# Two modulation vectors of the first attention: summed by TensorE from the weights in the ring instead of by VectorE

## The chip, the cores and the metric

The kernel runs on one core of one Trainium2 chip. The metric is the device time of one execution in microseconds, as the median of several runs. The engines are TensorE (PE, with its weight loads as PEld), VectorE (DVE), ScalarE (ACT), GpSimd (POOL) and SyncE (SP), which issues the weight DMAs.

## The reference

A sequence of 256 tokens of width 1024 goes through three layers. Each begins with an adaptive norm: a conditioning vector `c` times a weight matrix gives shift, scale and gate. What matters here is layer 0's attention (`nsa_mixer`) and the norm of layer 1 behind it.

```python
def adaln_norm(x, c, g, w_ada, b_ada):
    mod = jax.nn.silu(c) @ w_ada + b_ada
    shift, scale, gate = jnp.split(mod, 3, axis=-1)
    h = rms_norm(x, g) * (1.0 + scale[:, None, :]) + shift[:, None, :]
    return h, gate[:, None, :]
...
    o = gates[..., 0:1] * o_cmp + gates[..., 1:2] * o_slc + gates[..., 2:3] * o_win
    o = o.reshape(B, T, ATTN_WIDTH)
    return (o * jax.nn.silu(z)) @ w_out
```

The product `silu(c) @ w_ada` has one row. The kernel cuts it into 30 vectors of 512 columns ("ada" 0 to 29, six for each of five norms); ada 6 to 9 are shift and scale of the second norm.

## The kernel before, in words

**Weights.** SP brings every weight into a ring of six slots of 128 x 1024 float32 (512 KB), in the order of `plan.units`, and issues a load when the slot's former unit has been used. A weight of a large product is split by ACT (rounded part, the CAST) and DVE or POOL (rest, the subtraction), and TensorE makes three products from the parts: L574, L576 and L589, each 128 x 128 weights on 512 columns. In this text "a product" is one of these.

**Modulation vectors.** A vector takes four ring units of two 128-row chunks. `ada_step` does one chunk on DVE: ring times a scalar of `c_act`, added into the accumulator `ada_acc` (L698 for the first chunk, L704 for the others). After eight steps `ada_sum` on TensorE adds the accumulator over the partitions with four matmuls against a column of ones (L735). `ada_collect` on DVE then adds bias and gain. Vector 3 alone is made in another way: `ada_direct` multiplies 128 x 128 blocks of the ring, as stationary weights, by one column of `c_act` on TensorE (L757), two chunks for each of four column groups of each unit. A float32 matmul that is no transpose stands in the trace as two records, each with a weight load.

**The first attention** (`Attention`, with 32 items: 16 heads, two branches) goes in 16 pairs. In step p TensorE makes the scores of pair p (L1167, L1169), turns the probabilities of the two items of pair p-1 (L1176, three transposes each), weighs the values of pair p-2 (L1187 to L1189), and puts in products of the output gate ("nsa", 5), 28 of 48 over the attention; 20 are kept for behind it. DVE masks the scores and takes their maximum (L1218, L1220, from PSUM), makes the bias (L1199), copies every second turned item (L664), does ada steps, and every second step weighs a group of four (L1251, L1445, L1450). ACT makes the exponentials (L1244, L1246) and the other copies. POOL adds groups (L1608) and subtracts for the units of ("nsa", 5) (L533). Of the 32 ada steps of vectors 6 to 9, twelve are done ahead of the attention and twenty in it.

**Behind it** `by_halves` on TensorE takes the 20 kept products, turns the attention's output, and makes the first half of the output projection ("nsa_out", 0), with `ada_sum` of vectors 6 to 9 between groups of eight products. DVE collects the four vectors, then takes the residual (L864), then subtracts for the last two units of ("nsa_out", 1) (L533), for which TensorE's L589 wait.

Of the kernel before, what the change touches and what calls it, by code (L numbers as in the profile page):

```python
# [12 lines left out]
P = 128  # L13
# [3 lines left out]
KC = D // P  # L17
# [98 lines left out]
ADA_ON_PE = (3,)  # L116
# [3 lines left out]
class Plan:  # L120


    def __init__(self, stages):
# [8 lines left out]
        for kind, key, lots, freers in stages:  # L132
# [3 lines left out]
            for i, dmas in enumerate(lots):  # L136
                if kind == "ada_mix":
                    consumer = "pe" if key[i] in ADA_ON_PE else "ada"
                elif kind in ("beside", "beside_more"):
                    consumer = "ada" if key[i][0] == "ada" else "split"  # L140
# [13 lines left out]
            elif kind in ("beside", "beside_more"):  # L154
                for name in dict.fromkeys(key):
                    mine = [u for u, m in zip(units, key) if m == name]
                    self.outputs[name] = (None if name[0] == "ada" else len(self.freers), mine)
                    if name[0] == "ada":
                        self.ada_at.update((u, name[1]) for u in mine)
# [64 lines left out]
def first_stages(A):  # L224
# [37 lines left out]
    s.append(beside([(("nsa", 5), w, 2304)], range(8, 10), 2))  # L262
# [99 lines left out]
def build(nc, A, const_ap, out, last_block=2):  # L362
    ctx = ExitStack()
    with ctx:
# [17 lines left out]
        mod_tmp = sb("mod_tmp", [P, 4])  # L382
        mod_scale = sb("mod_scale", [P, 5, KC])
# [74 lines left out]
        mod_ready = sem("mod_ready")  # L458
        dve_chain = sem("dve_chain")
        act_chain = sem("act_chain")  # L460
# [223 lines left out]
        def ada_step(n, kk):  # L684
# [4 lines left out]
            if n >= SUMS and kk == 0 and n - SUMS not in ADA_ON_PE:  # L689
                dve.wait_ge(ada_summed, n - SUMS + 1 - sum(a < n - SUMS for a in ADA_ON_PE))  # L690
# [19 lines left out]
        def ada_beside(n0, i):  # L710

            n, kk = n0 + i // 8, i % 8
# [12 lines left out]
        def ada_sum(pe, n):  # L725
# [3 lines left out]
            if n >= SUMS:  # L729
                pe.wait_ge(mod_ready, TOGETHER[n][0] if n in TOGETHER else n)  # L730
# [32 lines left out]

        collected = [0]

        def ada_collect_up_to(n):
            while collected[0] < n:
                ada_collect(collected[0])

        def ada_collect(n):  # L770

            dve, link = nc.vector, chain["dve"]
            assert collected[0] == n, n
# [3 lines left out]
            if n in ADA_ON_PE:  # L777
# [4 lines left out]
            else:  # L782
                last = TOGETHER[n][-1] if n in TOGETHER else n
                dve.wait_ge(ada_summed, last + 1 - sum(a < last for a in ADA_ON_PE))
# [4 lines left out]
            elif part < 4:  # L789
                gain = cols[:, 0, 16 + 8 * layer + half.start:16 + 8 * layer + half.stop]  # L790
                if n in TOGETHER:
                    dve.wait_ge(mod_ready, n)
# [63 lines left out]
        def residual_half_dve(dve, layer):  # L856

            stage = RESIDUALS[layer]
            for tt in range(TT):
# [3 lines left out]
                dve.wait_ge(mod_ready, 6 * layer + 5)  # L863
# [18 lines left out]
        def residual_tile_dve(dve, layer, tt):  # L882
# [4 lines left out]
            dve.wait_ge(mod_ready, 6 * layer + 6)  # L887
# [82 lines left out]
        def shift_left_act(act, layer, tt, h):  # L970
            name, b = f"norm{layer + 1}", 2 * tt + h
            act.wait_ge(mod_ready, 6 * layer + 10)
# [144 lines left out]
        class Attention:  # L1117
# [27 lines left out]
            def pe(self, pe, products, n_products, lead=0):  # L1145

                n, done = len(self.items), 0
                for p in range(self.steps + 2):
                    for part in range(4):
# [3 lines left out]
                        if part % 2 == 0 and 0 <= j < n:  # L1153
                            self.turn_probs(pe, j)
# [169 lines left out]
        def nsa_dve(dve, link):  # L1324
# [48 lines left out]
            def some_ada(n):  # L1373
                for _ in range(n):
                    ada_beside(6, ada_done[0])
# [91 lines left out]
            def ada_in_attention(i):  # L1467
                some_ada(n_before + (32 - n_before) * (i + 1) // 32 - ada_done[0])
# [1517 lines left out]
```

## Time and profile before

| what | value |
|---|---|
| median of three runs | 1240.8 us (1237.46 to 1241.46) |
| profiled execution, its own time | 1239.51 us |
| its span in the profile | 1237.7 us |
| mean granted TensorE clock | 0.977 of full |
| busy: PE, DVE, ACT, POOL | 92%, 71%, 44%, 12% |

Busy shares are means over the whole span. A row of a timeline gives the start, how long the instructions took together, and in brackets the idle time ahead of them with what ended it. Matmuls overlap, so what one costs is read from start to next start, not from its duration.

### The profile page before, as it was taken

The numbers are of one execution on the slowest core, as the hardware profiler recorded it, in microseconds if no ns is written. First come the engines' busy times: TensorE is split into PE (matmuls) and PEld (weight loads), VectorE is DVE, ScalarE is ACT, GpSimd is POOL, SyncE is SP. The second block draws the span as 40 slices with busy tenths as digits, with TensorE's granted clock in tenths as the row PEclk, the third lists the DMA queues.
The fourth block names the chain that finished last, engine by engine and source line by source line (L and its number), as shares of the span: only waits on it lengthen the run. The fifth ranks groups of instructions, "written<-read, shape, count | busy, mean of one in ns | idle before, by whom it ended". The sixth has DMA issues, their size and how long they took to land. (4 is left out here: it accounts for less than half of the span.)

```text
span 1237.7 us, 19929 instructions
## 1 busy us (share of the span) xinstructions
PE 1135.5 (92%) x7662; PEld 954.1 (77%) x7662; DVE 874.1 (71%) x1458; ACT 549.9 (44%) x989; POOL 152.3 (12%) x109
## 2 busy tenths in 40 slices
PE   6878899899898899999989999898988998999997
PEld 5657677777677688888878877787878876888886
DVE  5866798589786699965489946847576656855554
ACT  1333366433363634344477754433141435434542
POOL 0010131122331100000000002104033021000011
PEclk9988899999899999999999999998989999999999
DMA  8875343378654399976455552751102144955452
GB/s 321 288 269 196 112 136 121 109 227 293 219 190 137 106 325 328 342 241 187 153 173 178 169 186 90 249 189 36 37 1 72 59 152 153 318 186 185 160 199 69
DMA packets 143513, 221.63 MB, mean 179 GB/s; under 512 B 10855, under 2 KB 66747, under 8 KB 143291
## 3 DMA queue, kind: packets, MB, share of 16 engines
q1 hardware_dynamic: 140512, 216.37, 53.2%
q10 hardware_dynamic: 2907, 4.00, 0.9%
q8 instruction: 61, 1.00, 0.3%
q14 instruction: 33, 0.27, 0.1%
HBM read 219.28 MB, written 1.05 MB: 178 GB/s over the span
## 5 line engine op out<-in xcount | busy, mean ns | idle before, releaser
L533 DVE TENSOR_TENSOR w_parts<-ring,w_parts 128x1024 fp32r<-128x1024 f32 (+2 forms) x276 | 341.9, 1275 | 90.6 <-ACT w_parts L528 89.8
L528 ACT CAST w_parts<-ring 128x1024 fp32r<-128x1024 f32 (+2 forms) x288 | 290.0, 1036 | 259.6 <-PE bank L576 70.6
L574 PE MATMUL bank<-w_parts,lhs_hi 128*128 128x512 f32 (+2 forms) x960 | 385.2, 402 | 13.6 <-ACT w_parts L528 9.2
L576 PE MATMUL bank<-w_parts,lhs_lo 128*128 128x512 f32 (+2 forms) x960 | 377.2, 393 | 0.0
L589 PE MATMUL bank<-w_parts,lhs_hi 128*128 128x512 f32 (+2 forms) x960 | 266.6, 394 | 18.1 <-DVE w_parts L533 18.1
L589 PEld LDWEIGHTS bank<-w_parts,lhs_hi 128*128 128x128 f32 x960 | 180.4, 191 | 58.8 <-DVE w_parts L533 25.2
L574 PEld LDWEIGHTS bank<-w_parts,lhs_hi 128*128 128x128 f32 x960 | 184.3, 192 | 51.8 <-issue 13.2
L576 PEld LDWEIGHTS bank<-w_parts,lhs_lo 128*128 128x128 f32 x960 | 184.3, 192 | 32.3 <-issue 0.2
L704 DVE SCALAR_TENSOR_TENSOR ada_acc<-ring,c_act,ada_acc 128x512 f32<-128x512 f32 x203 | 168.7, 831 | 13.3 <-DMA ring<-in_ada_w 3.0
L574 PE MATMUL bank<-w_parts,up_hi 128*128 128x512 f32 x176 | 68.7, 390 | 0.0
L576 PE MATMUL bank<-w_parts,up_lo 128*128 128x512 f32 x176 | 68.5, 389 | 0.0
L873 POOL TENSOR_TENSOR x<-x,xn 128x512 f32<-128x512 f32 x10 | 17.6, 1780 | 403.5 <-DVE xn L864 403.5
L651 PE MATMUL bank<-const,arena 128*128 128x128 f32 (+2 forms) x318 | 45.4, 275 | 11.2 <-DVE arena L664 5.1
L651 PEld LDWEIGHTS bank<-const,arena 128*128 128x128 f32 (+2 forms) x318 | 36.7, 141 | 18.9 <-DVE arena L664 5.8
L589 PE MATMUL bank<-w_parts,up_hi 128*128 128x512 f32 x176 | 48.4, 390 | 0.0
L1913 DVE TENSOR_TENSOR arena<-arena,bank 128x256 f32<-128x256 f32 x44 | 17.5, 417 | 39.3 <-ACT arena L1925 39.0
L2031 DVE SCALAR_TENSOR_TENSOR arena<-arena,cols 128x256 f32<-128x256 f32 x96 | 42.2, 481 | 2.3 <-ACT arena L2021 0.8
L1925 ACT ACTIVATE arena<-bank 128x256 f32<-128x256 f32 x44 | 16.3, 382 | 58.8 <-PE bank L589 57.5
L533 POOL TENSOR_TENSOR w_parts<-ring,w_parts 128x1024 fp32r<-128x1024 f32 x12 | 28.9, 2406 | 77.9 <-ACT w_parts L528 77.9
L1244 ACT ACTIVATE arena<-arena 128x128 f32<-128x128 f32 x48 | 19.3, 401 | 43.1 <-DVE arena L1199 40.8
L574 PEld LDWEIGHTS bank<-w_parts,up_hi 128*128 128x128 f32 x176 | 33.0, 188 | 6.8
L576 PEld LDWEIGHTS bank<-w_parts,up_lo 128*128 128x128 f32 x176 | 33.0, 188 | 6.8
(359 smaller groups left out, 1455.6 us busy)
## 6 DMA issues: line engine op xcount, KB each, us to landing
ring<-in_w_ffn_up SPq DMA_DIRECT2D x176, 256.0 KB, 4.2
ring<-in_w_ada SPq DMA_DIRECT2D x72, 512.0 KB, 4.9
ring<-in_ada_w SPq DMA_DIRECT2D x48, 512.0 KB, 4.9
ring<-in_w_ffn_down SPq DMA_DIRECT2D x44, 512.0 KB, 4.6
ring<-in_w_in SPq DMA_DIRECT2D x44, 512.0 KB, 4.5
ring<-in_dil_w_in SPq DMA_DIRECT2D x32, 512.0 KB, 4.6
ring<-in_nsa_w_in SPq DMA_DIRECT2D x20, 512.0 KB, 4.6
ring<-in_w_in SPq DMA_DIRECT2D x20, 416.0 KB, 4.2
```

What stands on the lines that cost most here:

```text
L528: eng.copy(hi, raw).then_inc(hi_ready, 1)
L533: eng.tensor_tensor(lo, raw, hi.bitcast(F32), ALU.subtract).then_inc(lo_ready[who], 1)
L574: pe.matmul(b, x_hi, w, start=(k0 + k == 0), stop=False)
L576: mm = pe.matmul(b, x_lo, w, start=False, stop=False)
L589: mm = pe.matmul(bank[2 * plan.pair[o] + tt][:, 0:n], x_hi, lo[:, k * n:(k + 1) * n], start=False, stop=last_k)
L651: mm = pe.transpose(bank_of_turn(i)[0:mout, col:col + kin], src, ident[0:kin, 0:kin])
L704: ins = dve.scalar_tensor_tensor(acc, w, s, acc, ALU.mult, ALU.add)
L873: pool.tensor_tensor(x[:, tt, A_HALF], x[:, tt, A_HALF], y_gated[:, tt, :], ALU.add).then_inc(x_half, 1)
L1244: act.activation(pr[:, 0:P], m[:, 0:P], ACT.Exp, bias=self.bias[:, i, 0:1], scale=SCALE, accum_out=self.den[:, i, 0:1])
L1913: dve.tensor_tensor(up_h[:, j % 2, tt, :], up_a[:, j % 2, tt, :], gemm_bank(name + "_up", j, tt)[:, 256:512], ALU.mult).then_inc(bank_free ...
L1925: act.activation(up_a[:, j % 2, tt, :], gemm_bank(name + "_up", j, tt)[:, 0:256], ACT.Silu).then_inc(silu_done, 1)
L2031: ins = dve.scalar_tensor_tensor(a, p[:, h, tap:tap + T], tap_weight(b, tap, h), a, ALU.mult, ALU.add)
```

## The change

Vectors 8 and 9 join vector 3 on TensorE. Their eight units keep their places in the ring's order, but their user is now TensorE. The 64 matmuls (two vectors, four units, four column groups, two chunks) are spread over the attention: two ahead of each of the 32 turns, behind the wait for the PSUM bank and ahead of the wait for the exponentials. Their sums stand in free columns of banks 2 and 3, and DVE reads them with two small reductions when the attention's last group has been added; TensorE waits for that (`direct_read`) ahead of ("nsa_out", 0). DVE loses sixteen ada steps, keeps four in the attention, and `ada_sum` of 8 and 9 is gone. The rest (`ready_count`, `summed_count`, removed semaphores) only counts anew.

```diff
-ADA_ON_PE = (3,)
+ADA_ON_PE = (3, 8, 9)
...
+        def ada_direct_product(pe, d):
+
+            n, i, c = 8 + d // 16, d % 16 // 4, d % 4
+            u = plan.outputs["ada", n][1][i]
+            if c == 0:
+                await_unit(pe, u)
+            for k in range(CHUNKS):
+                kk, at = CHUNKS * i + k, k * 512 + c * P
+                mm = pe.matmul(direct_columns(c % 2)[:, n - 8, c // 2, i:i + 1], ring[:, u % RING, at:at + P],
+                               c_act[:, kk:kk + 1], start=(k == 0), stop=(k == CHUNKS - 1))
+            if c == 3:
+                mm.then_inc(pe_units, 1)
+
+        def ada_direct_read(dve):
+
+            for parity in range(2):
+                dve.tensor_reduce(direct_sum.rearrange("p n (c o) -> p n c o", o=2)[:, :, :, parity],
+                                  direct_columns(parity), AX, ALU.add).then_inc(direct_read, 1)
...
-            def turn_probs(self, pe, j):
-                pe.wait_ge(self.exp_done, j + 1)
+            def turn_probs(self, pe, j, before_turn):
                 if j >= 2:
                     pe.wait_ge(self.probsT_ready[j % 2], j // 2)
+                if before_turn:
+                    before_turn(j)
+                pe.wait_ge(self.exp_done, j + 1)
...
             def ada_in_attention(i):
-                some_ada(n_before + (32 - n_before) * (i + 1) // 32 - ada_done[0])
+                some_ada(n_before + min(4, (i + 1) // 2) - ada_done[0])
...
             link(dve.tensor_tensor(o, o, o_part[:, last % 2, :, :, :], ALU.add))
+            ada_direct_read(dve)
             turned_left_dve(dve, "nsa_o", range(2))
...
             for _ in products:
                 pass
+            pe.wait_ge(direct_read, columns_read) if columns_read else None
...
-            nsa_att.pe(pe, products, 48 - BEHIND, lead=1)
+            nsa_att.pe(pe, products, 48 - BEHIND, lead=1, before_turn=lambda j: ada_direct_product(pe, j))
             by_halves(pe, "nsa_out", "nsa_o", 0, lambda tt, c: nsa_o[:, tt, 2 * c:2 * c + 2, :].rearrange("p h d -> p (h d)"),
-                      products, range(6, 10))
+                      products, (6, 7), 2)
```

On TensorE, one step in the middle of the attention stood so before (scores, then twice turn, product, values):

```order
304 L1167 MATMUL bank<-arena 128x128 x2
305 L1169 MATMUL bank<-arena 128x256 x2
306 L1176 MATMUL bank<-const,arena 128x128 x3
307 L1187 MATMUL bank<-arena 128x64
308 L1188 MATMUL bank<-arena 128x64
309 L1189 MATMUL bank<-arena 128x64
310 L1176 MATMUL bank<-const,arena 128x128 x3
311 L574 MATMUL bank<-w_parts,lhs_hi 128x512
312 L1187 MATMUL bank<-arena 128x64
```

The like step on TensorE in the changed kernel, where L1213 and L1215 are the scores, L796 the new products, L1224 the turns and L1235 to L1237 the values:

```order
345 L1213 MATMUL bank<-arena 128x128 x2
346 L1215 MATMUL bank<-arena 128x256 x2
347 L796 MATMUL bank<-c_act,ring 128x1 x2
348 L1224 MATMUL bank<-const,arena 128x128 x3
349 L595 MATMUL bank<-w_parts,lhs_lo 128x512
350 L1235 MATMUL bank<-arena 128x64
351 L1236 MATMUL bank<-arena 128x64
352 L1237 MATMUL bank<-arena 128x64
353 L796 MATMUL bank<-c_act,ring 128x1 x2
354 L1224 MATMUL bank<-const,arena 128x128 x3
```

Two matmuls of one column were put ahead of each turn; nothing else on TensorE moved in the attention.

On DVE, a step of the attention before, from the bias to the next mask (L1199 bias, L704 ada step, L664 copy):

```order
400 L1199 TENSOR_SCALAR arena<-arena 128x4
401 L704 SCALAR_TENSOR_TENSOR ada_acc<-ring,c_act,ada_acc 128x512
402 L664 COPY arena<-bank 128x384
403 L704 SCALAR_TENSOR_TENSOR ada_acc<-ring,c_act,ada_acc 128x512
404 L1218 ISA arena<-bank,const 128x128
```

The same place on DVE in the changed kernel, once without and once with the weighing of a group (L1247 bias, L683 copy, L1299 to L1498 weighing):

```order
194 L1247 TENSOR_SCALAR arena<-arena 128x4
195 L683 COPY arena<-bank 128x384
196 L1266 ISA arena<-bank,const 128x128
...
204 L1247 TENSOR_SCALAR arena<-arena 128x4
205 L683 COPY arena<-bank 128x384
206 L1299 RECIPROCAL arena<-arena 128x8
207 L1493 TENSOR_TENSOR arena<-arena 128x8
208 L1498 TENSOR_TENSOR xn<-bank,arena 128x512
209 L1266 ISA arena<-bank,const 128x128
```

The ada steps between bias and copy and behind the copy are gone from the fourth pair on.

On TensorE, in ("nsa_out", 0), the sums of vectors 8 and 9 before (L735):

```order
461 L735 MATMUL bank<-const,ada_acc 128x1 x4
462 L574 MATMUL bank<-w_parts,lhs_hi 128x512
463 L576 MATMUL bank<-w_parts,lhs_lo 128x512
464 L574 MATMUL bank<-w_parts,lhs_hi 128x512
465 L576 MATMUL bank<-w_parts,lhs_lo 128x512
466 L589 MATMUL bank<-w_parts,lhs_hi 128x512 x4
467 L735 MATMUL bank<-const,ada_acc 128x1 x4
```

The same products in the changed kernel, where the last sum (L756) stands ahead of them:

```order
487 L756 MATMUL bank<-const,ada_acc 128x1 x4
488 L608 MATMUL bank<-w_parts,lhs_hi 128x512 x4
489 L593 MATMUL bank<-w_parts,lhs_hi 128x512
490 L595 MATMUL bank<-w_parts,lhs_lo 128x512
491 L593 MATMUL bank<-w_parts,lhs_hi 128x512
492 L595 MATMUL bank<-w_parts,lhs_lo 128x512
493 L593 MATMUL bank<-w_parts,lhs_hi 128x512
494 L595 MATMUL bank<-w_parts,lhs_lo 128x512
495 L593 MATMUL bank<-w_parts,lhs_hi 128x512
496 L595 MATMUL bank<-w_parts,lhs_lo 128x512
497 L608 MATMUL bank<-w_parts,lhs_hi 128x512 x4
```

The projection's last sixteen products now run with no sum between or behind them.

## Rows read from the trace of the kernel before

**Rows 1.** The page, part 1: busy us, share, instructions of each engine

```profile
PE 1135.5 (92%) x7662; PEld 954.1 (77%) x7662; DVE 874.1 (71%) x1458; ACT 549.9 (44%) x989; POOL 152.3 (12%) x109
```

**Rows 2.** Windows: length, busy (count) of PE, PEld, DVE, ACT, POOL; clock, DMA

```profile
142.00:146.00 4.00, 4.00 (x19) 2.79 (x17) 2.75 (x12) 2.56 (x11) 0.00 (x0) 0.50 0.06 7
150.00:175.00 25.00, 22.94 (x187) 18.92 (x187) 23.19 (x86) 16.22 (x61) 6.13 (x4) 1.00 0.38 127
175.00:200.00 25.00, 21.34 (x174) 17.47 (x172) 23.82 (x81) 15.58 (x62) 8.47 (x5) 1.00 0.40 124
200.00:225.00 25.00, 25.00 (x149) 21.83 (x149) 15.86 (x25) 13.79 (x18) 1.26 (x1) 1.00 0.47 151
```

**Rows 3.** Timeline of PE, a step of the attention: start, us, instruction

```profile
159.13 0.49 PE L1167 MATMUL bank<-arena 64*128 64x128 f32 x4
159.45 0.60 PE L1169 MATMUL bank<-arena 64*128 64x256 f32 x4
...
160.96 0.48 PE L589 MATMUL bank<-w_parts,lhs_hi 128*128 128x512 f32 x1
161.27 0.49 PE L1176 MATMUL bank<-const,arena 128*128 128x128 f32 x3
...
162.59 0.49 PE L1167 MATMUL bank<-arena 64*128 64x128 f32 x4
```

**Rows 4.** Timelines of DVE and POOL: steps, bias and POOL's subtraction

```profile
139.45 0.98 DVE L1199 TENSOR_SCALAR arena<-arena 128x4 f32<-128x4 f32 x1
...
158.81 0.74 DVE L704 SCALAR_TENSOR_TENSOR ada_acc<-ring,c_act,ada_acc 128x512 f32<-128x512 f32 x1
...
161.89 2.92 DVE L704 SCALAR_TENSOR_TENSOR ada_acc<-ring,c_act,ada_acc 128x512 f32<-128x512 f32 x1
...
161.90 2.36 POOL L533 TENSOR_TENSOR w_parts<-ring,w_parts 128x1024 fp32r<-128x1024 f32 x1
...
193.12 2.92 DVE L704 SCALAR_TENSOR_TENSOR ada_acc<-ring,c_act,ada_acc 128x512 f32<-128x512 f32 x1
```

**Rows 5.** Timeline of PE: turns that waited, late in the attention

```profile
196.66 0.52 PE L1176 MATMUL bank<-const,arena 128*128 128x128 f32 x3 [0.51 <-DVE arena L664]
...
199.35 0.52 PE L1176 MATMUL bank<-const,arena 128*128 128x128 f32 x3 [1.55 <-ACT arena L664]
```

**Rows 6.** Timeline of PE: one-column matmuls, vector 3 and sums

```profile
20.00 6.97 PE L757 MATMUL bank<-c_act,ring 128*128 128x1 f32 x32
26.82 1.84 PE L735 MATMUL bank<-const,ada_acc 128*128 128x1 f32 x8
...
214.46 0.95 PE L735 MATMUL bank<-const,ada_acc 128*128 128x1 f32 x8
215.27 0.49 PE L574 MATMUL bank<-w_parts,lhs_hi 128*128 128x512 f32 x1
215.59 0.40 PE L576 MATMUL bank<-w_parts,lhs_lo 128*128 128x512 f32 x1
```

**Rows 7.** Timeline of PE: the attention's first turn

```profile
141.50 0.90 PE L1176 MATMUL bank<-const,arena 128*128 128x128 f32 x3 [1.02 <-ACT arena L1246]
```

**Rows 8.** The page, part 6: loads of vectors 6 to 11

```profile
ring<-in_ada_w SPq DMA_DIRECT2D x48, 512.0 KB, 4.9
```

**Rows 9.** Timelines of PE and DVE behind the attention

```profile
222.69 0.95 PE L735 MATMUL bank<-const,ada_acc 128*128 128x1 f32 x8
223.50 0.48 PE L574 MATMUL bank<-w_parts,lhs_hi 128*128 128x512 f32 x1
...
227.95 0.73 PE L589 MATMUL bank<-w_parts,lhs_hi 128*128 128x512 f32 x2 [0.53 <-DVE w_parts L533]
...
230.18 0.73 PE L589 MATMUL bank<-w_parts,lhs_hi 128*128 128x512 f32 x2 [0.58 <-DVE w_parts L533]
...
223.68 0.23 DVE L788 TENSOR_TENSOR mod_shift<-bank,cols 128x4 f32<-128x4 f32 x2 [5.74 <-PE bank L735]
...
224.75 1.29 DVE L864 TENSOR_TENSOR xn<-bank,gate_row 128x512 f32<-128x512 f32 x2
225.96 4.16 DVE L533 TENSOR_TENSOR w_parts<-ring,w_parts 128x1024 fp32r<-128x1024 f32 x2
```

More of the change, by code:

```diff
@@ L115, with ready_count, summed_count @@
 FIRST_CONST = 2 * P + 2
-ADA_ON_PE = (3,)
+ADA_ON_PE = (3, 8, 9)
+ADA_ORDER = tuple(range(30))
+def ready_count(n):
+    return ADA_ORDER.index(n) + 1
+def summed_count(n):
+    return sum(a not in ADA_ON_PE for a in ADA_ORDER[:ready_count(n)])
 class Plan:
@@ L139, in __init__ @@
                 elif kind in ("beside", "beside_more"):
-                    consumer = "ada" if key[i][0] == "ada" else "split"
+                    consumer = "split" if key[i][0] != "ada" else "pe" if key[i][1] in ADA_ON_PE else "ada"
                 slot = len(self.units) % RING
@@ L158, in __init__ @@
                     if name[0] == "ada":
-                        self.ada_at.update((u, name[1]) for u in mine)
+                        self.ada_at.update((u, name[1]) for u in mine if name[1] not in ADA_ON_PE)
                     else:
@@ L261, in first_stages @@
     s += [gemm("nsa", 4, w, 1792, 512, act), ada(6), ada(7)]
-    s.append(beside([(("nsa", 5), w, 2304)], range(8, 10), 2))
+    big = column_units([(w, 2304, 512)], 512, KC)
+    lots = {n: iter(ada(n)[2]) for n in (8, 9)}
+    small = (8, 8, 8, 8, 9, 9, 9, 9)
+    order, units = [], []
+    for i, unit in enumerate(big):
+        order += [("nsa", 5)] + [("ada", n) for n in small[2 * i:2 * i + 2]]
+        units += [unit] + [next(lots[n]) for n in small[2 * i:2 * i + 2]]
+    s.append(("beside", order, units, act))
     s += [gemm("nsa_out", j, o, 512 * j, 512, gated) for j in range(2)]
@@ L688, in ada_step @@
             acc = ada_acc[:, n % SUMS, :]
-            if n >= SUMS and kk == 0 and n - SUMS not in ADA_ON_PE:
-                dve.wait_ge(ada_summed, n - SUMS + 1 - sum(a < n - SUMS for a in ADA_ON_PE))
+            if kk == 0:
+                earlier = [a for a in range(n % SUMS, n, SUMS) if a not in ADA_ON_PE]
+                if earlier:
+                    dve.wait_ge(ada_summed, summed_count(earlier[-1]))
             k = kk % CHUNKS
@@ L729, in ada_sum @@
             if n >= SUMS:
-                pe.wait_ge(mod_ready, TOGETHER[n][0] if n in TOGETHER else n)
+                first = TOGETHER[n][0] if n in TOGETHER else n
+                pe.wait_ge(mod_ready, ready_count(first) - 1)
             acc = ada_acc[:, n % SUMS, :]
@@ L776, in ada_collect @@
             sums = sum_columns(n)[:, 0:4]
-            if n in ADA_ON_PE:
+            if n in (8, 9):
+                dve.wait_ge(direct_read, 2)
+                sums = direct_sum[:, n - 8, :]
+            elif n in ADA_ON_PE:
                 dve.wait_ge(pe_units, plan.units[plan.outputs["ada", n][1][-1]][2] + 1)
@@ L783, in ada_collect @@
                 last = TOGETHER[n][-1] if n in TOGETHER else n
-                dve.wait_ge(ada_summed, last + 1 - sum(a < last for a in ADA_ON_PE))
+                dve.wait_ge(ada_summed, summed_count(last))
             half = slice(4 * (part % 2), 4 * (part % 2) + 4)
@@ L1611, in nsa_pool, with by_halves @@
             rstd_pool(pool, 0)
-        def by_halves(pe, stage, name, ready, src, products, vectors):
+        def by_halves(pe, stage, name, ready, src, products, vectors, columns_read=0):
             for _ in range(8):
@@ L2593, in ada_steps @@
                     for step in range(sum(LEVEL_STEPS[r][:s]), sum(LEVEL_STEPS[r][:s + 1])):
-                        ada_beside(26 + r, step)
+                        ada_beside(26 + r + step // 8, step % 8)
                 for n, a in ORDER:
```

34 lines of the change are left out of this document (18 added, 16 removed).

## The prediction

> **What bounds the kernel now.** I read the busy shares of the page first: TensorE is busy 92% of the span and nothing else comes near [rows 1]. That is a mean, so I went to the windows around the change. In the attention two engines are nearly full: TensorE 22.94 and 21.34 of 25 us, VectorE 23.19 and 23.82 of 25 us; behind it TensorE is full, 25.00 of 25 us, and VectorE is not, 15.86 [rows 2]. So the attention is where a trade between the two engines has to be priced. The change makes VectorE cheaper and TensorE dearer there, and what decides is how much room TensorE has.
>
> That I read from TensorE's timeline, from start to start. A step with two products runs from 159.13 to 162.59, 3.46 us, with hardly a gap [rows 3]. The attention's steps from the fourth to the sixteenth take 3.76 us on average (I counted twelve starts of the scores, 148.98 to 194.15). The difference is waiting: 2.06 and 3.66 us in the two windows, 5.7 us in all [rows 2], of which the longest stand late, 0.51 and 1.55 us ahead of turns [rows 5]. A busy row's end is modelled and hides some 0.1 us at each of about eleven waits; so between 5.7 and 6.9 us, and I take 6.3. Much of it goes back to VectorE: an ada step takes 0.74 us, but 2.92 us where GpSimd's subtraction of 2.36 us starts at the same time [rows 4]; three steps in the attention are held up so, by 2.2 us each.
>
> **The sum, part by part.**
>
> VectorE loses sixteen ada steps, about 0.7 us each, and the three long ones among them: 16 x 0.7 + 3 x 2.2 = 18 us of its time. That is worth only as much as TensorE waited for it, the 6.3 us above. It needs no more than about 2.6 us for a step afterwards (3.5 less 0.9), against over 4 us of TensorE's.
>
> TensorE gets 64 matmuls, 128 records. The nearest row is the same operation for vector 3: 32 records from 20.00 to 26.82, 0.213 us each at half clock [rows 6], so 0.107 at full. The sums L735 have the same shape at full clock: eight records from 214.46 to 215.27, 0.81 us, and the next product starts 0.32 instead of 0.23 us before its successor, 0.90 us together, 0.112 each [rows 6]. I take 0.11: a group of four records ahead of a turn costs 0.44 us. The bounds are 0.10 (0.81 / 8) and 0.113.
>
> The Trainium skill, "TensorE: Matmul & The Clock Gate", section "Back-to-back issue gap", speaks for less: it gives about 81 ns for a sustained pair of weight load and matmul at 128 columns. By it the 128 records would cost 10.4 us (an estimate) instead of 14.1, and the net result below would be about 3.5 us lower. The rows of this trace have 0.10 to 0.11 us even for one column, and I go by them.
>
> At full clock stand 28 groups (items 4 to 31): 28 x 0.44 = +12.3 us. They fill the waits: -6.3 us. TensorE then needs 3.4 + 0.9 = 4.3 us for a step. The chain that it could still wait for is scores, mask, bias, exponentials, turn: it begins 0.85 us into the step and takes about 2.5 us, and the turn of these items comes one step later, behind the next scores and the new products, at 4.3 + 0.85 + 0.44 = 5.6 us. So two microseconds are in hand. Three times GpSimd's subtraction may now catch the bias L1199 instead of an ada step; the first bias of the attention shows what that does, 0.98 us for an instruction of 128 x 4 [rows 4]. Up to 2.3 us of delay against 2 us in hand: +0.4 us in all for the three.
>
> The first groups run at half clock: TensorE's granted clock is 0.50 from 142 to 146, and there it is busy 4.00 of 4 us [rows 2]. The first group costs nothing, since the first turn waits 1.02 us for the exponentials [rows 7] and the group takes 0.85. The next two cost 0.85 each and the fourth 0.44: +2.1 us. Without the low clock it would be 1.3.
>
> Loads: the units keep their places; a load takes 4.9 us to land [rows 8] and each is issued at least two steps (over 8 us) ahead of its first new product, apart from the first ones, which are in the ring ahead of the attention. Nothing for that. In the other direction, TensorE frees unit 8.0 after item 3 and the last at item 31, before the projection wants the slot.
>
> Attention together: 12.3 - 6.3 + 0.4 + 2.1 = +8.5 us.
>
> Behind it two sums go: from the start of the last sum to the first product after it 0.81 us, and 0.09 for that product's late successor, 2 x 0.90 = -1.8 us, in a stretch where TensorE has no gap [rows 2, 9]. Then a second gain: VectorE sat 5.74 us until the sum of vector 9 was there, collected for 1.07 us, and only at 224.75 took the residual, whose input had been ready at about 222.7 [rows 9]. Behind the residual are its subtractions, 4.16 us for two, and TensorE waited for these 0.53 and 0.58 us (start to start 1.4 us over the usual) [rows 9]. Now the collect waits for vector 7 alone, some 4 us earlier, the residual begins with the end of the projection's half, about 1.3 us earlier against TensorE's own clock, and both waits fall below their margin: -1.4 us. The two reductions (at most 0.25 us each, from the 0.23 us of two L788 [rows 9] and more elements) lie ahead of the turned left side, which has 0.8 us in hand; the new wait of TensorE for them is met 1.5 us ahead. Queued behind them on VectorE are the rests of the left side and the subtractions, and these have the same room. Later stages see only a shift.
>
> Sum: +8.5 - 1.8 - 1.4 = +5.3 us. On the profiled execution's 1239.5 us that is 1244.8; on the median of the runs, 1.3 us higher, 1246.1. I give 1245.5.
>
> **The rivals.**
>
> *Nearly even.* TensorE's clock was low because it had stood idle around 137 to 141.5; the first group now works there, so the clock may rise a microsecond or more sooner, and with 0.10 instead of 0.11 us a record the groups give back 28 x 0.04 = 1.1 us. With 1.3 us from the clock and the 6.9 us of waits that makes 5.3 - 1.1 - 1.3 - 0.6 = +2.3 us, 1243 us.
>
> *Faster.* VectorE is the real pace, at 23.2 and 23.8 of 25 us busy, and one-column products hide in the turns' waits and behind streaming products. Then steps go at the best pace seen, 3.4 us: 12 x 0.36 = -4.3, the two waits of rows 5 -2.1, behind the attention -3.2: -9.6 us, 1231 us. Against it stands that TensorE has no gap in such a step [rows 3]. It decides where a group costs less than 0.12 us.
>
> *GpSimd's port.* The Trainium skill, "SBUF — State Buffer" (its part on the shared port pair), says GpSimd and VectorE take this pair as an exclusive lock and the second waits for the whole instruction; rows 4 agree, with 2.92 us instead of 0.74. Worked out from the rows: if the bias is caught at all three subtractions and the delay of 2.2 us goes through, +6.6 us on the sum less the 0.4 counted, 1252 us. For it: there is no ada step left to be caught in its place. Against it: the 2 us in hand.
>
> **How the numbers follow.** Forecast 0.50, nearly even 0.30, faster 0.13, port 0.07. A measurement here tells about 0.3%, 3.7 us, from no change. The forecast's own range is 1244.5 to 1249.5: group costs of 0.40 to 0.46 us, waits of 5.7 to 6.9 us, the port up to 1.5 us. The nearly even case reaches from 1237.5 to 1244.5. The range 1237.5 to 1249.5 leaves out the last two cases. Slower 0.57 (forecast and port), same 0.30, faster 0.13.
>
> **What would show it.** Right: the new products at 0.11 us a record; steps of 4.2 to 4.4 us; TensorE busy over 24.5 of 25 us in the attention; VectorE under 17 of 25; in the projection no L589 waiting for L533. Wrong: steps of 3.9 us or less (cheaper products or a false count of waits); turns waiting over 1 us for exponentials behind a long L1247 (port); the clock up before 146 us (nearly even); a wait for a ring unit on the new products.

## The result and the profile after

| what | before | after |
|---|---|---|
| median of four runs each | 1240.95 us (1237.46 to 1241.46) | 1270.9 us (1264.07 to 1292.44) |
| profiled execution, its own time | 1239.51 us | 1292.44 us |
| its span | 1237.7 us | 1290.6 us |
| mean granted TensorE clock | 0.977 | 0.929 |

The ratio is 1.0229, 95% interval 1.015 to 1.0309; it leaves out, as all ratios here do, executions more than 1.5% above the fastest of their kernel. In these four executions the change is slower, by over five times the forecast amount and far outside the range; the interval lies above 1, but on both sides of 2%. The four executions already tell that one number does not describe the kernel: 1264.07, 1264.39, 1277.41 and 1292.44 us, at mean clocks of 0.954, 0.955, 0.946 and 0.929. The slower ones are those with the lower clock.

The page of the profiled execution of the changed kernel, its first part and the row of the granted clock in 40 slices:

```profile
PE 1202.3 (93%) x7774; PEld 1018.0 (79%) x7774; DVE 861.2 (67%) x1444; ACT 551.6 (43%) x989; POOL 152.3 (12%) x109
...
PEclk9988655589999989999999999988999999999999
```

TensorE has 66.8 us more to do than in [rows 1], for 112 more records. Nothing of that size was added: 128 new records at the forecast 0.11 us are 14 us. The clock row shows the rest. Slices five to eight, from 129 to 258 us, are at 0.5 to 0.6; that is the attention. Windows of the changed kernel from there (columns as in [rows 2]: length, busy (count) of PE, PEld, DVE, ACT, POOL; clock, DMA):

```profile
140.00:144.00 4.00, 2.74 (x16) 1.92 (x15) 3.28 (x13) 1.57 (x7) 2.35 (x1) 0.70 0.00 0
144.00:148.00 4.00, 4.00 (x20) 3.18 (x18) 2.23 (x9) 2.53 (x11) 0.00 (x0) 0.50 0.02 4
148.00:152.00 4.00, 4.00 (x21) 3.54 (x17) 1.37 (x9) 1.35 (x5) 0.00 (x0) 0.50 0.44 131
200.00:204.00 4.00, 4.00 (x20) 3.22 (x19) 0.56 (x1) 1.92 (x5) 0.00 (x0) 0.50 0.40 131
260.00:264.00 4.00, 4.00 (x21) 4.00 (x21) 1.62 (x3) 3.97 (x5) 0.32 (x1) 0.50 0.30 67
264.00:268.00 4.00, 4.00 (x15) 3.61 (x15) 1.99 (x7) 0.44 (x1) 0.00 (x0) 0.51 0.17 65
268.00:272.00 4.00, 4.00 (x23) 3.37 (x23) 1.95 (x3) 1.08 (x2) 0.00 (x0) 1.00 0.00 0
```

Before, the clock fell at the same place, behind short idle times of TensorE at the attention's start (0.91 and 1.25 us), and was back within 7 us: [rows 2] have 0.50 at 142 to 146 and 1.00 from 150 on. Now it falls at the same place and stays at 0.50, the lower level of 1.2 GHz, up to about 268 us, some 126 us long, with TensorE busy 4.00 of 4 us in each window. Here it comes back when the attention is over and 512-column products stream again. What it does to a step stands in TensorE's timeline, one step of the changed kernel from scores to scores:

```profile
203.09 1.06 PE L1215 MATMUL bank<-arena 64*128 64x256 f32 x4
204.08 1.01 PE L796 MATMUL bank<-c_act,ring 128*128 128x1 f32 x4
204.96 0.88 PE L1224 MATMUL bank<-const,arena 128*128 128x128 f32 x3
205.49 0.78 PE L595 MATMUL bank<-w_parts,lhs_lo 128*128 128x512 f32 x1
206.06 0.52 PE L1235 MATMUL bank<-arena 128*128 128x64 f32 x2
206.38 0.63 PE L1236 MATMUL bank<-arena 128*128 128x64 f32 x2
206.80 0.63 PE L1237 MATMUL bank<-arena 128*128 128x64 f32 x2
207.23 0.96 PE L796 MATMUL bank<-c_act,ring 128*128 128x1 f32 x4
...
211.05 1.06 PE L1215 MATMUL bank<-arena 64*128 64x256 f32 x4
```

The step takes 7.96 us, with no idle time in it. Each row costs about twice what it did: the four new records start 0.88 us ahead of the turn, 0.22 us each, where [rows 6] have 0.213 for vector 3 (half clock by this pace; the trace records the clock only from 48 us on). Nothing waits; the step is twice a full-clock step of 4.0 to 4.3 us. From the first scores to the first kept product the attention takes 126.6 us (139.25 to 265.84), against 65.3 before (137.3 to 202.6): +61 us. Of this 8.5 were forecast. At the end of the span 52.9 us of it are left.

The Trainium skill, "TensorE: Matmul & The Clock Gate", section "What's actually happening", says that activity releases the throttle, and its section "HAM oscillation — how this bites in real kernels" that idle gaps bring it back. The fall behind idle time is in line with this, though the profiles of four other kernels below show like gaps and no fall; 126 us at 0.50 with a TensorE that the trace shows as busy throughout are not.

### The profile page after: what moved, and what is told of

Read it like the earlier page. It is cut to its first block and busy times, and to the rows that moved or that the text cites. A ratio compares the mean times of both kernels' runs of the same rounds, so it can differ in the third digit from the quotient of the medians.

```text
span 1290.6 us, 20106 instructions
## 1 busy us (share of the span) xinstructions
PE 1202.3 (93%) x7774; PEld 1018.0 (79%) x7774; DVE 861.2 (67%) x1444; ACT 551.6 (43%) x989; POOL 152.3 (12%) x109
## 5 line engine op out<-in xcount | busy, mean ns | idle before, releaser
L552 DVE TENSOR_TENSOR w_parts<-ring,w_parts 128x1024 fp32r<-128x1024 f32 (+2 forms) x276 | 342.3, 1277 | 87.8 <-ACT w_parts L547 86.9
L608 PE MATMUL bank<-w_parts,lhs_hi 128*128 128x512 f32 (+2 forms) x960 | 268.3, 396 | 16.4 <-DVE w_parts L552 16.4
L608 PEld LDWEIGHTS bank<-w_parts,lhs_hi 128*128 128x128 f32 x960 | 181.6, 192 | 55.6 <-DVE w_parts L552 22.2
L725 DVE SCALAR_TENSOR_TENSOR ada_acc<-ring,c_act,ada_acc 128x512 f32<-128x512 f32 x189 | 151.1, 799 | 14.8 <-DMA ring<-in_ada_w 3.5
L683 DVE COPY arena<-bank 128x384 f32<-128x384 f32 (+1 forms) x33 | 19.5, 591 | 55.2 <-PE bank L1224 49.7
L608 PE MATMUL bank<-w_parts,up_hi 128*128 128x512 f32 x176 | 48.5, 390 | 0.0
L796 PEld LDWEIGHTS bank<-c_act,ring 128*128 128x128 f32 x128 | 31.4, 327 | 10.5 <-issue 9.8
```

What stands on the lines that cost most here:

```text
L552: eng.tensor_tensor(lo, raw, hi.bitcast(F32), ALU.subtract).then_inc(lo_ready[who], 1)
L608: mm = pe.matmul(bank[2 * plan.pair[o] + tt][:, 0:n], x_hi, lo[:, k * n:(k + 1) * n], start=False, stop=last_k)
L683: return eng.tensor_copy(dst, src) if eng is nc.vector else eng.copy(dst, src)
L725: ins = dve.scalar_tensor_tensor(acc, w, s, acc, ALU.mult, ALU.add)
L796: mm = pe.matmul(direct_columns(c % 2)[:, n - 8, c // 2, i:i + 1], ring[:, u % RING, at:at + P], c_act[:, kk:kk + 1], start=(k == 0), stop ...
```

## The experiments

Twelve kernels, in the order in which they ran. The medians of the kernel before, run beside them, are 1240.07 to 1240.33 us, and none of its 89 executions there took more than 1247.2 us. The first four kernels ran on one chip, the next four on a second, the last four on a third; a comparison within one of these groups is the safer one.

**VectorE's relief alone.** VectorE without its sixteen steps, TensorE with a quarter of the new matmuls (the expectation says what is left out):

```diff
-            for k in range(CHUNKS):
+            for k in range(CHUNKS - 1, CHUNKS) if c >= 2 else ():
```

> The changed kernel with 16 of its 64 new matmuls (48 left out, so vectors 8 and 9 are not computed). VectorE's relief is whole. Clock theory (the changed kernel loses because the granted clock stays at 0.50 through the attention): with little new work the clock rises near 147 us as before, the steps run at about 3.5 us, and the time is 1230 to 1236 us. Theory that the loss comes from VectorE's side (waits that the moved sums or the new read bring): the time stays above 1255 us.

Measured: 1243.96 us (1236.45 to 1248.72, ten executions), ratio 1.0022 [0.9995, 1.005]. Both expected times were missed. The clock is at 1.00 through the attention, so the long low stretch is not VectorE's doing; but the gain is not there either, though VectorE is down to 19.35 of 25 us and TensorE has only 32 new records. DVE's and POOL's timelines of this kernel show one reason:

```profile
165.09 2.13 DVE L1247 TENSOR_SCALAR arena<-arena 128x4 f32<-128x4 f32 x1
...
164.84 2.36 POOL L552 TENSOR_TENSOR w_parts<-ring,w_parts 128x1024 fp32r<-128x1024 f32 x1
```

The bias, 0.17 us at other places, starts while GpSimd's subtraction runs and ends with it at 167.2. It is caught so at all three subtractions (2.13, 2.38 and 2.38 us). Behind the first two a step takes 4.7 us instead of 3.5; the third falls into the last step. Before, an ada step stood in the bias's place and was caught instead [rows 4].

**The same weight loads, more columns.** Each new matmul keeps its stationary weights from the ring and moves 128 columns of the identity instead of one:

```diff
-                mm = pe.matmul(direct_columns(c % 2)[:, n - 8, c // 2, i:i + 1], ring[:, u % RING, at:at + P],
-                               c_act[:, kk:kk + 1], start=(k == 0), stop=(k == CHUNKS - 1))
+                mm = pe.matmul(bank[2 + c % 2][:, 3 * P:4 * P], ring[:, u % RING, at:at + P],
+                               ident, start=(k == 0), stop=(k == CHUNKS - 1))
```

> The changed kernel with the same 64 weight loads from the ring, but 128 moving columns (the identity) instead of one; vectors 8 and 9 are not computed. At 0.11 us a record the 128 columns should cost no time of their own. Clock theory: what holds the clock down is that the new matmuls have one moving column; the clock rises in the first steps, the steps take 4.0 to 4.2 us, and the time is 1240 to 1247 us. Theory of load work (more work on TensorE holds the clock or costs the time whatever moves through it): the time stays at 1260 us or more.

Measured: 1240.32 us (1237.83 to 1243.51, ten), ratio 1.0 [0.9975, 1.0026]. No execution was long. The steps take 4.34 to 4.41 us at full clock, apart from those with a caught bias; with one column they take 4.25 to 4.32 in the two kernels that follow. So the columns cost some 0.1 us a step, about 1.5 us in all (an estimate from these steps), which the medians do not show. In the profiled execution the clock did not fall at the attention's start at all, so it does not tell whether it would have come back; the kernels with the gap do.

**Fills around the first scores.** The changed kernel with eight and three matmuls of 256 columns on constants, whose results nothing uses, behind the first and second scores, to fill the time in which TensorE stood:

```diff
+                            if fills and p < 2:
+                                fill(pe, bank[7], fills[p])
```

> The changed kernel with 8 idle matmuls of 256 columns behind the first scores and 3 behind the second, into a free bank, so that TensorE does not stand idle between 137 and 141.5 us. Theory that the clock only has to be kept up once: it stays at 1.00 through the attention, 1238 to 1246 us. Theory that the attention with the one-column matmuls cannot hold it: it falls some microseconds later and the time is as that of the changed kernel, 1260 to 1290 us.

Measured: 1243.99 us (1237.84 to 1261.99, ten), ratio 1.0017 [0.9993, 1.0042]. In the profiled execution the clock is 1.00 from 140 on, in spite of the one-column products; windows of this kernel:

```profile
140.00:144.00 4.00, 3.73 (x21) 3.12 (x22) 2.77 (x10) 1.51 (x5) 2.35 (x1) 1.00 0.01 4
...
150.00:175.00 25.00, 24.31 (x206) 21.38 (x207) 16.72 (x69) 13.41 (x53) 4.86 (x3) 1.00 0.44 147
175.00:200.00 25.00, 24.18 (x205) 21.05 (x205) 16.40 (x69) 13.41 (x52) 6.15 (x4) 1.00 0.28 86
```

The steps take 4.25 to 4.32 us, the forecast step of 4.3, apart from two of 5.1 at caught biases. One execution of ten took 1261.99 us at a mean clock of 0.963: by its time and clock the fall came in it, so the fills do not exclude it.

**TensorE's share alone.** The kernel before, with VectorE as it was, and 64 one-column matmuls from constants ahead of the turns:

```diff
+                if self.name == "nsa_att":
+                    for k in range(2):
+                        pe.matmul(bank[2 + j % 2][:, 3 * P + j // 2:3 * P + j // 2 + 1],
+                                  const[:, P * k:P * (k + 1)], c_act[:, k:k + 1], start=(k == 0), stop=(k == 1))
```

> The kernel before with 64 one-column matmuls added at the places of the changed kernel, their weights from the constants; VectorE keeps all its steps. Clock theory: the clock stays low for the attention, and the time is 1262 to 1295 us, at least that of the changed kernel. Theory that it is the changed kernel's other edits: 1242 to 1250 us, from 14 us of new work into 6 us of waits.

Measured: 1242.54 us (1237.04 to 1299.43, ten), ratio 1.0019 [0.9984, 1.0054]. The profiled execution ran at full clock, with steps of 4.31 us and TensorE at 25.00 of 25 us in both windows. That is the step of the changed kernel, without VectorE's relief. In it the clock did not fall at the attention's start, though TensorE had the idle times of before there (0.91 and 1.26 us). I had expected a low clock in every execution, and eight of ten did not have it. Two took 1296.1 and 1299.4 us at a mean clock of 0.929, the clock and nearly the time of the changed kernel's longest: by this the one-column matmuls can do it alone, from weights that never change. The ratio is that of the eight; no profile shows a long one.

**The changed kernel again**, unchanged, to see how its executions spread.

> The changed kernel unchanged, on the chip of the other runs of this call. The runs so far have shown that with one-column matmuls an execution either keeps its full clock into the attention (steps of 4.3 us, about 1237 to 1246 us) or falls near 140 us and stays low (up to 1290 to 1300 us). Theory of a clock that falls by chance and is then not lifted: executions of both kinds and in between, more of the low ones than with the 128-column form. Theory that the changed kernel always loses 20 us or more: none under 1255 us.

Measured: median of twelve 1279.28 us. The executions, sorted: 1238.6, 1244.2, 1250.0, 1250.8, 1265.8, 1267.3, 1291.3, 1292.4, 1293.2, 1293.2, 1293.7, 1294.8 us, with clocks from 0.978 (the first) and 0.973 (the second) down to 0.929 to 0.932 (the last six). So it is one kernel with many times, and a longer time goes with a lower mean clock. The four quickest alone give a ratio of 1.0042 [1.0004, 1.0081]. At its best it runs within the spread of the kernel before. The profiled one was again low through the attention, from 142.4 to 268.7 us.

**A fall on purpose.** To compare kernels behind a like fall, fourteen linked copies on VectorE ahead of the first mask keep TensorE idle for 6.7 us at one place. The kernel before, the changed kernel, and the changed kernel with wide products each got them:

```diff
+                        for _ in range(14 if p == 0 and self.name == "nsa_att" else 0):
+                            link(dve.tensor_copy(left_tmp[:, 0, :], left_tmp[:, 0, :]))
```

The wide form here computes all vectors: the column of `c_act` is repeated, and the result's first column is the wanted one.

```diff
+            r = d // 2
...
-                mm = pe.matmul(direct_columns(c % 2)[:, n - 8, c // 2, i:i + 1], ring[:, u % RING, at:at + P],
-                               c_act[:, kk:kk + 1], start=(k == 0), stop=(k == CHUNKS - 1))
+                mm = pe.matmul(bank[2 + c % 2][:, 3 * P + r:4 * P], ring[:, u % RING, at:at + P],
+                               c_act[:, kk:kk + 1].broadcast_to([P, P - r]), start=(k == 0), stop=(k == CHUNKS - 1))
```

> The kernel before with 14 linked copies of 128 x 512 on VectorE ahead of the attention's first mask, so that TensorE stands idle some 7 us longer behind the first scores, and its clock falls in every execution. Clock theory: it rises again within two or three steps, since the steps of before have no one-column work; the time is 1245 to 1253 us. Rival (whatever attention follows, a clock that has fallen there stays low): 1285 us or more.

> The changed kernel with the same 14 copies. Clock theory: the clock falls in every execution and is not lifted while the one-column matmuls run, so 1290 to 1310 us, mostly at the upper end, 45 us or more over the kernel before with the copies. Rival (the low stretch is not tied to the new matmuls): as the kernel before with the copies, plus at most 8 us.

> The changed kernel with the 14 copies, and with the column of c_act given 113 to 128 times as moving operand, each result staying in its own column of the bank; all vectors are computed. Clock theory, with what moves through the array as the cause: the clock rises within a few steps, steps of 4.3 to 4.4 us, 1247 to 1258 us. Rival (the number of weight loads holds the clock down, not what moves): as the changed kernel with the copies, 1290 us or more.

Measured: before with the gap 1245.56 us (1239.98 to 1250.58, ten), ratio 1.0038 [1.0018, 1.0059]; wide with the gap 1247.52 us (1242.61 to 1250.07, ten), ratio 1.0047 [1.0027, 1.0067]; changed with the gap 1279.77, 1280.68, 1300.91 and 1301.19 us, in all four of its executions (1290 to 1310 had been expected). Windows of the kernel before with the gap, of the wide kernel with it, and of the changed kernel with it:

```profile
144.00:148.00 4.00, 2.16 (x12) 1.52 (x12) 3.02 (x15) 1.87 (x8) 0.00 (x0) 0.50 0.00 0
148.00:152.00 4.00, 4.00 (x22) 2.87 (x21) 2.86 (x14) 2.23 (x9) 0.00 (x0) 0.64 0.10 15
152.00:156.00 4.00, 4.00 (x37) 3.52 (x36) 3.10 (x17) 2.24 (x9) 0.00 (x0) 1.00 0.34 120
```

```profile
148.00:152.00 4.00, 4.00 (x18) 3.47 (x19) 1.65 (x11) 1.99 (x9) 0.00 (x0) 0.51 0.02 4
152.00:156.00 4.00, 4.00 (x36) 3.58 (x36) 2.59 (x13) 2.20 (x10) 0.00 (x0) 1.00 0.45 131
160.00:180.00 20.00, 19.39 (x161) 16.45 (x161) 14.03 (x54) 10.70 (x41) 5.20 (x4) 1.00 0.48 159
```

```profile
152.00:156.00 4.00, 4.00 (x20) 3.12 (x18) 1.48 (x5) 2.33 (x9) 0.00 (x0) 0.50 0.00 0
160.00:180.00 20.00, 20.00 (x92) 17.28 (x92) 6.70 (x26) 6.58 (x23) 1.26 (x1) 0.50 0.31 106
200.00:220.00 20.00, 20.00 (x93) 17.09 (x93) 6.35 (x27) 6.58 (x23) 1.93 (x2) 0.50 0.09 27
220.00:240.00 20.00, 20.00 (x140) 17.82 (x140) 10.40 (x45) 8.93 (x36) 4.19 (x3) 0.81 0.24 80
224.00:228.00 4.00, 4.00 (x21) 3.31 (x22) 0.68 (x2) 1.31 (x5) 0.00 (x0) 0.56 0.78 262
228.00:232.00 4.00, 4.00 (x36) 3.54 (x35) 2.74 (x13) 2.23 (x9) 0.00 (x0) 1.00 0.00 0
```

All three fall to 0.50. Without the products and with wide ones the clock is back by 152 us. With one-column products it is still at 0.50 at 220 us, and TensorE's PE row is full all that time. In this execution, one of the two shorter ones, it comes back at 227.5 us, after 82 us and inside the attention, while each step still has its one-column products; the steps then take 4.3 us. So these products delay the return, and do not rule it out. The wide and the changed kernel with the gap ran on one chip; they have the same number of matmuls, the same weight loads and the same places; only the moving columns differ. The busy share in the rows does not tell the two apart.

**The wide form without the gap.** The same edit of the product, no copies.

> The changed kernel with the column of c_act given 113 to 128 times as moving operand, all vectors computed, without the copies. Clock theory: no execution over 1250 us, steps of 4.35 us, and 0 to 5 us over the kernel before in the median. Rival (the load work itself holds the clock in some executions): a part of them over 1260 us, as with the changed kernel.

Measured: 1240.04 us (1237.54 to 1245.77, twelve), ratio 0.9992 [0.9974, 1.0011]. This small edit has the time of the kernel before and not the spread of the changed one; the changed kernel's 1279 us were measured on another chip, and the like comparison on one chip is that with the gap. Its profile has a short fall and the return, with no copies:

```profile
147.00:151.00 4.00, 3.64 (x18) 3.11 (x20) 2.24 (x11) 2.98 (x14) 0.00 (x0) 0.57 0.02 4
151.00:155.00 4.00, 4.00 (x36) 3.52 (x34) 2.59 (x12) 2.44 (x10) 0.00 (x0) 1.00 0.46 131
```

The clock was low from 147.3 to 150.7 us. Two steps take 5.1 instead of 4.35 us, at caught biases; the third catch is in the last step.

**GpSimd behind the bias.** GpSimd waits for the pair's bias before it subtracts, at the three places, first in the kernel with the relief alone, then in the wide one:

```diff
+                if grp in (2, 4, 6):
+                    pool.wait_ge(nsa_att.bias_ready, 2 * grp + 3)
                 stream_to("pool", units[grp // 2])
```

> The kernel with 16 of the 64 new matmuls (vectors 8 and 9 not computed), and GpSimd's second, third and fourth subtraction in the attention now wait until the bias of the step has been made, so that they no longer stand in its way. Port theory (what VectorE's relief is worth is lost because the subtraction catches the bias instead of an ada step): three waits of 1.1 us go, steps of 3.5 us on average, 3 to 5 us less than with 16 matmuls alone, 1236 to 1240 us. Rival (relief is worth nothing because something else paces the steps): as before, 1241 to 1245 us.

> The form with the repeated moving column, all vectors computed, with GpSimd's wait for the bias. Port theory: the three steps of 5.1 us become 4.35 us, 2.2 us less than without the wait, 1238 to 1242 us. Rival: the later subtraction makes TensorE wait for a low part, no gain or a loss.

Measured: relief alone 1240.07 us (1230.78 to 1245.52, twelve), ratio 0.9985 [0.9962, 1.0007], against 1243.96 without the wait; wide 1237.01 us (1235.18 to 1241.53, twelve), ratio 0.9977 [0.996, 0.9994], against 1240.04. The medians differ by 3.9 and 3.0 us. The first pair ran on two chips; the second ran on one, but the intervals of its ratios overlap. The rows are firmer: the two steps of 5.1 us are now 4.39 and 4.33, the last step is 0.86 us shorter, 2.4 us together, and in the kernel with the relief alone the average step falls from 3.82 to 3.61. POOL's timeline of the wide kernel, and DVE's around the first of these places:

```profile
166.67 2.38 POOL L552 TENSOR_TENSOR w_parts<-ring,w_parts 128x1024 fp32r<-128x1024 f32 x1 [0.28 <-DVE arena L1248]
...
166.43 0.17 DVE L1248 TENSOR_SCALAR arena<-arena 128x4 f32<-128x4 f32 x1
...
167.83 0.56 DVE L683 COPY arena<-bank 128x384 f32<-128x384 f32 x1 [1.24 <-PE bank L1225]
```

The bias is over in 0.17 us, and GpSimd waits 0.28 us for it; no step got longer by this. This kernel computes everything, and its median is 3.3 us under that of the kernel before, 0.2%; that is less than one measurement tells, but its interval excludes 1.

**One-column products only later.** None for items 0 to 7, twice as many for 8 to 15, one group from 16 on, with the gap's copies: the products start when the clock is back.

```diff
+            def late_products(j):
+                if 8 <= j < 16:
+                    for c in (j % 2, j % 2 + 2):
+                        ada_direct_product(pe, 4 * ((j - 8) // 2) + c)
+                elif j >= 16:
+                    ada_direct_product(pe, j)
```

> The changed kernel with one-column matmuls and the 14 copies that make the clock fall, but the products begin with item 8 (two groups ahead of each of the items 8 to 15, one from item 16 on); all vectors computed. Theory that one-column work does not lift a low clock but does not lower a high one: the clock is back before item 8, near 152 us, and stays; 1245 to 1256 us. Rival (the attention with one-column work cannot hold a high clock either): it falls again and the time is over 1270 us.

Measured: 1263.31 us (1262.19 to 1287.35, four), ratio 1.0175 [1.0146, 1.0205], between the 1245 to 1256 us of the idea and the rival's 1270 or more. The idea failed; windows of this kernel:

```profile
156.00:160.00 4.00, 4.00 (x36) 3.19 (x33) 3.16 (x15) 2.88 (x12) 0.00 (x0) 1.00 0.00 0
160.00:164.00 4.00, 3.94 (x34) 3.25 (x33) 2.97 (x15) 3.20 (x12) 1.28 (x1) 1.00 0.80 261
164.00:168.00 4.00, 4.00 (x32) 3.96 (x31) 1.74 (x8) 2.50 (x11) 0.00 (x0) 0.83 0.17 22
168.00:172.00 4.00, 4.00 (x19) 2.91 (x19) 2.44 (x10) 0.00 (x0) 3.05 (x2) 0.50 0.32 116
200.00:210.00 10.00, 10.00 (x46) 8.94 (x46) 4.72 (x16) 2.48 (x10) 3.58 (x2) 0.50 0.00 0
210.00:220.00 10.00, 10.00 (x70) 8.80 (x70) 4.42 (x21) 4.42 (x18) 0.99 (x1) 0.78 0.35 107
```

The clock was back at 1.00 from 153, and fell to 0.50 at about 167, some three microseconds after the first double group at 163.34. TensorE had idled 0.06 us in the two windows from 160 to 168. With the double groups gone and single ones left it was back at 214.5, ahead of the attention's end. So it seems that one-column products can also bring the clock down, not only keep it down, where they stand twice as thick (one profiled execution; two others have its time within 1 us); at the changed kernel's own spacing the profiled executions that began the attention at full clock (the fills, and TensorE's share alone) kept it throughout.

## Why the prediction was wrong

**What bounds.** Right. TensorE sets the step, and VectorE is no longer near it.

**The failing step** is "The first groups run at half clock", +2.1 us. It took the low stretch's end from the trace of before and priced the new products at half clock only up to there, as if they changed nothing about when the clock returns. They do: while one-column products stand in every step, it may return 82 us later, or not before the attention ends. In the profiled execution the whole attention runs at half clock. The attention's growth there is +61 us instead of +8.5, and the executions between (1250 to 1277 us) have mean clocks between those of the two ends. The three kernels with the gap show that the one moving column is the cause of the late return, and the two long executions of the kernel with TensorE's share alone, by their time and mean clock, that neither the ring nor VectorE's part is needed. What decides in an execution whether the clock falls and when it returns is open: the same program gave 1238.6 and 1294.8 us on one chip, and with like idle times at the attention's start (0.91 and 1.26 us) some profiled executions show the fall and others do not.

That the measured direction is the forecast one is luck. It was forecast from the groups' cost at full clock, and in the forms and executions that stay at full clock the change is within 0.5% of the kernel before (ratios 1.0017 with the fills, 0.9992 wide, 1.0042 for the four quickest of the changed kernel).

The rival "nearly even" went by the same reasoning in the other direction, that the first group fills idle time and the clock "may rise a microsecond or more sooner". It expected work of any kind to count. That rival and the forecast shared the mistake, so the range had no room for it.

**The sum at full clock** holds where it can be read. *Groups:* the four records take 0.36 to 0.47 us from start to next start in the kernel with TensorE's share alone; forecast 0.44. *Step:* 4.25 to 4.32 us with the fills where no bias is caught, 4.40 as an average of twelve; 4.31 there; forecast 4.3. *Waits:* TensorE at 25.0 of 25 us there, but at 24.3 and 24.2 with the fills, under the forecast 24.5, by the caught biases. *Ring and loads:* no new product waits for a unit in the profile after, as forecast.

**The port** was priced too low, at +0.4 us in all. Two steps of 5.1 instead of 4.35 us and a last step 0.86 us longer are 2.4 us, and the medians with GpSimd's wait are 3 to 4 us lower. What I called two microseconds in hand was some 1.4, the delay less what the step grew: the bias is late by 2.0 to 2.2 us, and then the exponentials and ScalarE's copy are late for the turn. The kernel with the relief alone has the turn's wait in TensorE's timeline:

```profile
168.66 0.55 PE L1224 MATMUL bank<-const,arena 128*128 128x128 f32 x3 [1.14 <-ACT arena L683]
```

The rival "GpSimd's port" had the mechanism right, all three biases caught, and its +6.6 us too high. The Trainium skill, "SBUF — State Buffer", section "SBUF: two separate sides", says that the shared pair is an exclusive lock for the whole instruction; the rows agree, the bias ends within 0.04 us of the subtraction. In the changed kernel at half clock the biases took 1.1 to 1.6 us and no step was longer than 8.07 us, caught bias or not, so it cost nothing visible there.

**VectorE's relief** was worth less than it seemed. I counted 6.3 us of TensorE's waits as filled. In the kernel with the relief alone TensorE still does not run at 3.5 us a step but at 3.82 (3.76 before), in part because the relief takes away the ada steps that GpSimd's subtraction used to catch, and the bias is caught in their place. With GpSimd behind the bias that step is 3.61, near the full step of [rows 3] with the two records a step that this kernel adds, 3.46 + 0.22.

**Behind the attention** the forecast of -1.8 and -1.4 us holds. TensorE's and DVE's timelines of the changed kernel, where [rows 9] show before:

```profile
278.69 0.95 PE L756 MATMUL bank<-const,ada_acc 128*128 128x1 f32 x8
...
281.44 0.95 PE L756 MATMUL bank<-const,ada_acc 128*128 128x1 f32 x8
...
282.43 0.23 DVE L834 TENSOR_TENSOR mod_shift<-bank,cols 128x4 f32<-128x4 f32 x2 [0.26 <-PE bank L756]
...
285.75 1.29 DVE L910 TENSOR_TENSOR xn<-bank,gate_row 128x512 f32<-128x512 f32 x2 [2.17 <-PE bank L608]
```

There are two sums instead of four, the collect starts 0.26 us after the last, and VectorE is idle for 2.17 us until the projection's half is there, instead of taking the residual late. No L608 has a wait in its row between 285 and 295 us; one starts some 0.2 us late (291.18). As a check by like products: between the 101st product of L574 and the 151st (at 210.8 and 260.8 us of before) the profiles of the changed, the wide and the gapped wide kernel gain 4.7 us on before. The two kernels that keep all four sums, with TensorE's share alone and before with the gap, gain 1.5 there; before has a short low spell in that stretch (249.4 to 252.8) and all these have none. The difference is the forecast 3.2 us.

**The total at full clock** came out below the sum. The profile with the fills is 9.5 us behind before at the 151st product, and 3.0 of these were there when the attention began. The other 6.5, with the fills' own time in them (the first step takes 4.54 us instead of 2.21), are close to the 5.3 that the sum gives up to here. At the end only 2.4 of the 9.5 are left. 1.8 go by 333 us, at the norm and the loads behind it, where the kernel before with the gap gives back 2.0 as well. 1.7 go in small pieces up to 821 us, and 3.7 in layer 2's many small products between 858 and 970 us. There the profile with TensorE's share alone gives back 4.3 us, the fastest kernel's 4.7, the wide one without the wait 0.9, and before with the gap none. They differ in where short low spells of the clock lie: one of 6.8 us, from 905 or 912 us, in before and in those that give back little, and two of 3.4 us, from 909 to 911 and from 926 to 928, in the others. That fits but was not tried. So that the full-clock form is about even with before is measured, and why it is not 5 us slower stays partly open.

## What to carry over

A matmul of one moving column costs nearly as much as one of 128 here, but TensorE's clock behaves otherwise under it: spread through a stage, such matmuls can keep the engine at 1.2 GHz, once it has fallen there, for as long as the stage lasts. Repeating the column over 113 to 128 moving columns took that away here, for about 0.1 us a step. When work leaves one engine, ask not only who was waiting for it but also what its instructions shielded: here the ada steps stood where GpSimd's subtraction struck, and without them it struck the bias on the critical chain. And before taking a granted clock from the trace of before into a sum, ask whether the change alters the work that the clock answers to, and look at several executions, not one.

## What the runs showed of the hardware that was not expected

- The granted clock stayed at 0.50 for about 126 us (82 us in one execution) with TensorE's row at 4.00 of 4 us in the windows read, and was back after 10.2 us, by 152 us, behind a longer idle time when the same products moved 113 to 128 columns.
- In one kernel it fell from 1.00 to 0.50 at about 167 us with TensorE busy 3.94 and 4.00 of 4 us.
- One program on one chip ran from 1238.6 to 1294.8 us, with mean clocks from 0.978 to 0.930.
- Behind idle times of 0.91 and 1.26 us at the attention's start the clock fell to 0.50 in some profiled executions (changed, wide) and not in others (TensorE's share alone, wide columns of the identity).
- An instruction of 128 x 4 on VectorE, 0.17 us alone, took up to 2.38 us beside GpSimd's 2.36 us subtraction, while a copy from PSUM (L683) inside GpSimd's 2.38 us kept its 0.56 us (167.83 in the fastest kernel).
- Four records with 124 moving columns take 0.55 us to the next start in the fastest kernel (160.69 to 161.24), four with one column 0.47 in the kernel with TensorE's share alone (160.91 to 161.38), and the whole steps are nearly equal, 4.33 to 4.40 and 4.25 to 4.32 us.
